# Two transformer blocks on one core: the second layer's modulation weights wait for the first layer's expert sums

## The reference

```python
for i in range(DEPTH):                      # DEPTH = 2
    mods  = sc  @ ada_w[i] + ada_b[i]       # sc = silu(c), scc = silu(c_ctx): the inputs c, c_ctx only
    cmods = scc @ ada_w[i] + ada_b[i]
    x, xc = layer(x, xc, mods, cmods, ...)

# layer:
h2 = rms_norm(x_new, n2) * (1 + sc2) + sh2
x_new = x_new + g2 * expert_choice_ffn(h2, router, w_gate, w_up, w_down)

# expert_choice_ffn: every one of 16 experts takes its best tokens, and its rows are added up by token
return jax.vmap(lambda ib, yb: jnp.zeros((t, d), yb.dtype).at[ib.reshape(-1)].add(yb.reshape(-1, d)))(idx, y)
```

## Time and profile before

| | us |
|---|---|
| median of 3 runs | 3906.89 (3906.81 to 3909.35) |
| the profiled execution | 3902.73 |
| its span in the trace | 3900.9 |
| PE busy in the span | 3302.3 (85%) |
| DMA, mean over the span | 163 GB/s |

### The profile page before, as it was taken

How to read it: one execution, slowest core, us unless ns; L and a number is a source line. 1 busy time by engine, 2 the same in 40 slices (tenths; PEclk the granted TensorE clock), 3 DMA queues, 4 the chain that set the end, 5 groups by cost and what they waited for, 6 DMA issues and landing times. The chain is left out here.

```text
span 3900.9 us, 41076 instructions
## 1 busy us (share of the span) xinstructions
PE 3302.3 (85%) x16972; PEld 1921.7 (49%) x16972; DVE 1055.7 (27%) x2000; ACT 659.3 (17%) x1275; POOL 440.3 (11%) x636
## 2 busy tenths in 40 slices
PE   3799998479999938999758777479998998879997
PEld 0456773323333303577332111168785586748875
DVE  0225542321111122443130000132324266222232
ACT  0111120100000111111100000032222155122231
POOL 1006700011111110170001111100000000000000
PEclk7896558589999968855869999889999979989998
DMA  9131000369999891100249999912312100132130
GB/s 393 39 97 44 1 0 11 140 234 389 385 388 391 308 374 54 65 1 1 78 172 413 414 412 412 371 54 87 108 58 97 65 1 1 65 113 87 65 119 27
DMA packets 141428, 637.02 MB, mean 163 GB/s; under 512 B 11824, under 2 KB 19008, under 8 KB 86000
## 3 DMA queue, kind: packets, MB, share of 16 engines
q1 hardware_dynamic: 121104, 575.58, 37.4%
q0 software_dynamic: 20192, 59.58, 5.0%
HBM read 611.95 MB, written 23.17 MB: 163 GB/s over the span
## 5 line engine op out<-in xcount | busy, mean ns | idle before, releaser
L897 PE MATMUL bank<-slots,HT 128*32 128x512 f32 x4096 | 479.1, 600 | 79.3 <-DMA slots<-in_w_up_dram 41.5
L667 PE MATMUL bank<-slots,HT 128*128 128x512 f32 (+2 forms) x960 | 400.7, 578 | 20.4 <-ACT done_mark L1531 20.4
L897 PEld LDWEIGHTS bank<-slots,HT 128*32 128x32 f32 x4096 | 121.7, 110 | 400.8 <-issue 243.4
L667 PEld LDWEIGHTS bank<-slots,HT 128*128 128x128 f32 x960 | 182.4, 192 | 230.3 <-issue 204.5
L667 PE MATMUL bank<-hT_high,chunk_high 128*128 128x512 f32 x704 | 277.3, 394 | 8.3 <-DVE low_slots L1922 8.3
L667 PE MATMUL bank<-hT_high,low_slots 128*128 128x512 f32 x704 | 277.7, 395 | 0.0
L667 PE MATMUL bank<-hT_low,chunk_high 128*128 128x512 f32 x704 | 276.9, 393 | 0.0
L916 PE MATMUL bank<-arena,HT 128*32 128x512 f32 x2048 | 243.9, 596 | 26.7 <-DMA arena<-in_w_down_dram 26.2
L698 PE MATMUL bank<-ident,arena 128*128 128x128 f32 x272 | 61.0, 402 | 223.0 <-DVE arena L1593 145.5
L667 PE MATMUL bank<-HT,slots 128*128 128x512 f32 (+1 forms) x480 | 172.3, 521 | 1.7 <-ACT done_mark L1531 1.7
L698 PEld LDWEIGHTS bank<-ident,arena 128*128 128x128 f32 x272 | 50.2, 212 | 237.5 <-issue 198.8
(11 more groups left out here) (323 smaller groups left out, 4431.0 us busy)
## 6 DMA issues: line engine op xcount, KB each, us to landing
slots<-in_w_gate_dram SPq DMA_DIRECT2D x128, 1024.0 KB, 8.6
slots<-in_w_up_dram SPq DMA_DIRECT2D x128, 1024.0 KB, 11.0
arena<-in_w_down_dram SPq DMA_DIRECT2D x128, 1024.0 KB, 13.2
slots<-in_ada_w_dram SPq DMA_DIRECT2D x24, 2048.0 KB, 22.2
slots<-in_w_in_dram SPq DMA_DIRECT2D x15, 2048.0 KB, 13.0
slots<-in_ffn_w_gate_dram SPq DMA_DIRECT2D x10, 2048.0 KB, 8.5
slots<-in_ffn_w_up_dram SPq DMA_DIRECT2D x10, 2048.0 KB, 8.8
slots<-in_ffn_w_down_dram SPq DMA_DIRECT2D x10, 2048.0 KB, 7.8
```

Of the source, the lines that this page charges most:

```text
L667: mm = pe.matmul(out_, lhsT, rhs, start=(n == 0), stop=(n == len(pairs) - 1))
L897: mm = pe.matmul(bank[32 * j:32 * j + 32, 2 + n, :], xT[:, kk0 + kk, lo:lo + 32], w[n][:, kk, 512 * h:512 * h + 512], start=(pair == 0 and ...
```

## The change

SP gets two waits ahead of the first load of the second layer's `ada`: for the last even and the last odd tile of `moe_rows` that `combine` of the first layer loads (48 on each semaphore, three tiles of 16).

```diff
             for stage in stages:
+                if stage.name == "combine":
+                    combined = [(sem[name], stage.at(name, stage.signals[name])) for name in ("moe_rows0", "moe_rows1")]
+                if stage.name == "ada" and stage.layer:
+                    for name, value in combined:
+                        sp.wait_ge(name, value)
                 for j, (make, (b, use)) in enumerate(stage.units):
                     unit = stage.first_unit + j
                     load(unit, make(slot_of(unit)))
```

## The result

| | before | changed |
|---|---|---|
| median | 3907.26 us (3906.81 to 3909.35, 4 runs) | 3930.47 us (3928.07 to 3932.13, 4 runs) |
| profiled execution | 3902.73 us | 3930.16 us |
| its span | 3900.9 us | 3928.4 us |

The ratio is 1.0058, with a 95% interval of 1.004 to 1.0075. The kernel is 23.2 us slower, 0.6%, where 22.6 us were forecast.

What follows compares the result with a forecast made beforehand. The chain scatter, combine, angles, bias was taken to bound the kernel, the modulation stream having 12.6 us to spare. A stage end 16.0 us later plus 6.6 in the tail gave +22.6, 3929 us from the median; range 3919 to 3941.

Steps and rivals of the forecast that it cites:

- step 2: POOL's mods and first combine tile, loaded without the modulation stream: 7.3 us from issue to use instead of 16.2.
- step 3: The other combine tiles: the sixth lands 15.4 us behind the first tile's start, today 26.6, releasing SP at 1396.9.
- C: Rival: the chain combine, angles, bias ends 25 us earlier and the stream isn't in its way; 3882 us, 2%.
- D: Rival: PE's clock in a later stage, attention of layer 1, falls out differently; around 3880 us, 3%.
- Steps 1 to 3: Up to SP's release: scatter alone 7.7 us, first tile 7.3, other tiles 15.4; release at 1396.9, 45.6 us later.
- Step 4: Modulation stream starts over: 8.7 us to first unit, 54.7 for eleven steps, 3 for POOL's loads; last unit 1463.3.
- Step 5: DVE from last unit to end of ada: 4.0 us plus 0.7 for the open clock; stage end 16.0 us later.
- Step 6: Mods' store and load before the norm share the engines with w_in: 17.2 us instead of 10.6, +6.6.
- How the two queues share: POOL beside the modulation stream gets less than a third of the bytes; with half, about 1.5 us less.
- A: Rival: the tail after ada is not stretched by w_in; 16.0 us alone, 3923 us, 12%.
- B: Rival: combine is no faster when alone, SP is released near 1417; +42 us, 3949 us, 8%.
- E: Rival: the wait doesn't bite because SP reaches it late or the count is met before; no change, 2%.

Runs made afterwards that it cites:

- the early bias: Bias and norm gains issued in the stage angles, in both kernels: 3927.4 us on the changed kernel, 3900.39 us on the kernel before.
- bias_early_after: Changed kernel with bias and norm gains of the second layer's ada issued in the stage angles: 3927.4 us against 3906.82 for the kernel before.
- hold_longer: Changed kernel with the second layer's w_in held until the second norm's mods have landed: 3922.72 us against 3905.82 for the kernel before.
- hold_w_in: Changed kernel with the second layer's w_in held until the first norm's mods have landed: 3925.88 us against 3906.82 for the kernel before.
- scatter_only: Changed kernel with the modulation loads released when the expert stage has ended on POOL: 3914.14 us against 3906.82 for the kernel before.
- four_early: Changed kernel with the wait before the fifth modulation unit instead of the first: 3914.07 us against 3906.82 for the kernel before.

## Why the prediction was right, point by point

Counted from the last expert's last DVE step on both sides:

| step | forecast | measured |
|---|---|---|
| 1. last scatter, issue to mark | 7.7 us | 6.2 |
| 2. issue of the mods to the first tile's use | 7.3 | 7.6 |
| 3. first tile to SP's release | 15.4 | 15.5 |
| release, from the last expert's step | 32.7 | 31.8 |
| 4. release to first unit | 8.7 | 8.2 |
| 4. first to last unit | 57.7 | 59.1 |
| 5. last unit to the end of `ada` | 4.7 | 4.05 |
| 6. end of `ada` to the norm's first step | 17.2 | 16.8 |
| to the norm's first step, against before | +22.6 | +21.6 |

The single steps are off by up to 1.5 us, some too long and some too short, so part of the agreement is errors that cancel. Two slips in the working did not touch the forecast: the later bound of the release, 1417, is what comes out if neither step 2 nor step 3 gets faster (with half of step 2 it is 1413), and the chances of C and D add up to 5%, not 4.

*What bounds the kernel.* That the chain through the gains set the time before, with the stream ready 12.6 us sooner, is shown by the early bias: 5 us in the kernel before, nothing in the changed one.

*Steps 1 to 3.* Steps 1 and 3 rested on rows from elsewhere in the trace, an earlier scatter and a tile of layer 1's `combine`; step 2 was an estimate from bytes and came within 0.3 us. Only the scatter was over-priced, by 1.5 us, since the one I took it from still had other transfers beside it for its first 5 us (a window from 1320 to 1325 has a DMA share of 1.01, the next 0.29).

*Step 4.* Undisturbed units came 4.97 us apart, as in layer 0. The term that was too small was the one added for POOL's share: the eleven steps took 4.4 us more than 11 x 4.97, not 3. That the tables, bias and gains cost all of it is not shown. In bias_early_after, where they had been issued by 1405, one step late in the stretch (1433.99 to 1440.24) is still 6.25 us long, and the whole stretch is as long as here, 59.2 us.

*Step 5.* Which clock the last unit would meet was open: it took 1.92 us in the changed kernel's trace, and 3.4 to 3.5 in four of the five experiments on it. I had added half the difference, and that the trace shows the short one is luck; with the long one the step is 5.5 to 5.7 us, not 4.7.

*Step 6.* This came from reading layer 0 as a model of what layer 1 would become, and hold_longer confirms the size of the whole as a difference: 5 to 6 us.

*How the two queues share.* I had set the row, less than a third of the bytes for POOL, against half of them by even turns of packets of one size. The packets are not of one size. The profile's counts of the two queues (q1 are SP's transfers, q0 POOL's; packets, MB, share), the mods and tiles under the stream in the kernel before (1383 to 1393), and then the mods of the first norm beside `w_in` in the changed kernel, from 1480 to 1483 and from 1483 to 1488:

```profile
q1 hardware_dynamic: 377, 2.88, 68.7%
q0 software_dynamic: 358, 1.34, 32.9%
...
q1 hardware_dynamic: 578, 1.16, 105.3%
...
q0 software_dynamic: 288, 1.05, 53.6%
q1 hardware_dynamic: 291, 0.57, 30.1%
```

Where both queues move, the packets come in nearly equal numbers, 358 to 377 and 288 to 291. So the trace, by the packets that the profile counts, agrees with the even turns of packets that the Trainium skill states (DMA: Bandwidth & Descriptors, Queues, rings and completion order). The bytes follow from the packets' size: 3.7 KB against 7.6 KB under the modulation stream, a third for POOL; 3.6 KB against 2.0 KB beside `w_in`, two thirds for POOL. So in the tail POOL does not lack its share. Its mods took 8.75 us beside `w_in` (1479.49 to 1488.24) and 5.65 in hold_w_in (1474.63 to 1480.28), and most of the difference stands ahead of the first packet: POOL issues at 1479.49, and from 1480 to 1483 only SP's packets move, while in hold_w_in the first ones move at 1475.5 to 1476.0. Why the first packet comes so much later beside a full queue, no run shows. The term of step 6 held because it was taken whole from layer 0, where the same order has the same delay in it.

*The rivals.* A (no shared tail) is refuted by the 16.8 us of step 6, and by hold_w_in, whose tail is 6 us shorter. B (`combine` no faster alone) is refuted by 17.9 us against 29.0, and by scatter_only, where it is 28.9 again. C would have needed the last unit through PE by about 1441; it started at 1467.6, which is 1463.4 on that clock. D did not happen: attention's clock is unchanged (0.55 over 260 us in both), and from the start of `conv_in` on the traces differ by 1.2 us. What I wrote there of the cause is not borne out, though: in rows 10 PE counts as busy for 20.00 of 20 us and its clock is 0.50 all the same. What keeps it there stays open. E is refuted by SP's first load at 1400.2.

What I had not put down is the second norm's load. It was no term of the forecast, since `w_in` was through by then, but hold_w_in ran into it.

## What to carry to other kernels

When a wait keeps a bulk stream back to let small transfers through, price the stream's new end: the moment at which the wait ends plus the bytes that are left then. The time for which the DMA engines stood idle is lost, and what the small transfers win counts only as far as they are still the later chain. A second place in the same program where the same code runs without the disturbance (here layer 0 and layer 1's `combine`) was a good price list: 3.7 us for a tile came out as 3.7, 17.2 us for the tail as 16.8. And if a bulk stream is to be held at all, hold the one that nobody needs yet (`w_in`), just as long as the small transfers on the critical chain take (10.8 us won here in the kernel before), and look where the next small transfer lies.

## What the runs showed that I had not expected

The same sixteen matmuls on the last unit took 1.9 us or 3.4 to 3.5 us from one trace to the next, though in the changed kernel, hold_w_in, hold_longer and bias_early_after the last five steps were 4.92 to 4.99 us each. The granted clock over the stream is 0.71 to 0.82 in the windows, a mean of the two levels, and which unit meets which level changes between executions. It is worth 1.4 to 1.6 us at the end of this stage.

A kernel's own profiled execution can lie 4 us from its median, and a good half of it has a row. `conv_in` of layer 0, 320 matmuls that both kernels run alike, took 103.4 us in the trace of before, with a clock of 1.00 in its first 10 us, 105.7 in that of the changed kernel, with 0.77, and 106.4 in four_early, with 0.70. That is 2.3 of the 4.2 us by which the changed kernel's trace was late at the last expert's step. Differences of this size are read from segments, not from spans.
